# A hybrid RWKV-7 / differential-attention layer: norm weights spread by TensorE, norms and the last store in halves, scores and half a block moved in the hand-written order

## What is computed

```python
h = rmsnorm(x) * norm_mix_pre            # (544, 1024)
c = h @ w_in                             # RWKV-7 columns | q k v | two gates
A  = rwkv7(c_a)                          # token shift, decay, per-chunk matrix state
Bd = diff_attn(q, k, v)                  # 4 heads, two softmaxes per head, causal in chunks of 64
mix = sigmoid(g_a) * (A @ w_out_a) + sigmoid(g_b) * (Bd @ w_out_b)
x = x + rmsnorm(mix @ w_o) * norm_mix_post
u_g, u_v = split((rmsnorm(x) * norm_ffn_pre) @ w_ffn_in)
x = x + rmsnorm((silu(u_g) * u_v) @ w_ffn_out) * norm_ffn_post
```

## Time and profile before

| | |
|---|---|
| runs, median of three | 1002.26 us |
| profiled execution, its own time | 1004.91 us |
| its span, first to last instruction | 1003.1 us |
| mean granted TensorE clock | 0.996 |
| PE busy | 959.4 us (96%) |
| POOL busy | 549.9 us (55%) |
| DVE busy | 450.6 us (45%) |
| ACT busy | 290.3 us (29%) |
| dense matmuls in the chain that ended last | 71% of the span |

### The profile page before, as it was taken

How to read it: one execution, slowest core, us unless ns; L and a number is a source line. 1 busy time by engine, 2 the same in 40 slices (tenths; PEclk the granted TensorE clock), 3 DMA queues, 4 the chain that set the end, 5 groups by cost and what they waited for, 6 DMA issues and landing times.

```text
span 1003.1 us, 23249 instructions
## 1 busy us (share of the span) xinstructions
PE 959.4 (96%) x9424; PEld 910.9 (91%) x9424; DVE 450.6 (45%) x870; ACT 290.3 (29%) x828; POOL 549.9 (55%) x595
## 2 busy tenths in 40 slices
PE   5999999999999899889999989999999999999996
PEld 4999899988878787778899989999999999999996
DVE  5456688467744445455466653333333333100003
ACT  5225265245564233432313541111111111111101
POOL 6667899634354243243469325555555555656671
PEclk9999999999999999999999999999999999999998
DMA  8333322332223111150046322223322223223232
GB/s 252 93 86 84 85 63 72 114 109 76 78 67 93 39 47 35 55 208 28 28 122 217 94 64 63 84 85 91 95 84 84 84 85 96 81 80 95 80 95 90
DMA packets 138306, 89.76 MB, mean 89 GB/s; under 512 B 5514, under 2 KB 130160, under 8 KB 138224
## 3 DMA queue, kind: packets, MB, share of 16 engines
q1 hardware_dynamic: 129604, 73.17, 25.7%
q10 hardware_dynamic: 8620, 15.42, 4.3%
HBM read 79.39 MB, written 9.19 MB: 88 GB/s over the span
## 4 chain that ended last, share of the span: by engine, by line
PE 86%; DVE 6%; ACT 4%; POOL 2%; issue 2%; DMA 1%; ACTq 0%; DVEq 0%; SPq 0%; POOLq 0%
PE dense L1069 71%; PE side L1149 3%; PE side L1192 1%; PE side L1218 1%; POOL w_lo L770 1%; PE side L1270 1%; PE side L977 1%; PE side L910 1%; DMA xs<-in_x_prompt 1%; PE side L896 1%; POOL w_hi L765 1%; PE side L951 1%; DVE gain L1731 1%; DVE h_lo L1724 0%; PE side L1242 0%
## 5 line engine op out<-in xcount | busy, mean ns | idle before, releaser
L765 POOL TENSOR_SCALAR w_hi<-w_raw 128x256 fp32r<-128x256 f32 (+1 forms) x255 | 155.6, 629 | 348.7 <-PE dense L1069 331.1
L770 POOL TENSOR_TENSOR w_lo<-w_raw,w_hi 128x256 fp32r<-128x256 f32 (+1 forms) x255 | 323.0, 1288 | 9.8
L1069 PE MATMUL dense<-h_hi,w_hi 128*128 128x272 f32 (+2 forms) x1376 | 297.8, 295 | 2.9 <-DVE h_lo L1724 1.5
L1069 PE MATMUL dense<-h_hi,w_lo 128*128 128x272 f32 (+2 forms) x1376 | 289.3, 289 | 0.0
L1069 PE MATMUL dense<-h_lo,w_hi 128*128 128x272 f32 (+2 forms) x1376 | 288.4, 288 | 0.0
L1069 PEld LDWEIGHTS dense<-h_hi,w_hi 128*128 128x128 f32 x1376 | 217.8, 189 | 12.4 <-issue 6.9
L1069 PEld LDWEIGHTS dense<-h_lo,w_hi 128*128 128x128 f32 x1376 | 218.4, 189 | 0.0
L1069 PEld LDWEIGHTS dense<-h_hi,w_lo 128*128 128x128 f32 x1376 | 217.4, 189 | 0.0
L1069 PE MATMUL dense<-S,w_hi 128*128 128x272 f32 (+2 forms) x648 | 109.3, 289 | 0.0
L1069 PEld LDWEIGHTS dense<-S,w_hi 128*128 128x128 f32 x648 | 92.1, 188 | 0.3 <-issue 0.2
L1069 PE MATMUL dense<-S,w_lo 128*128 128x272 f32 (+2 forms) x324 | 68.2, 288 | 0.0
(11 more groups left out here) (286 smaller groups left out, 1345.4 us busy)
## 6 DMA issues: line engine op xcount, KB each, us to landing
w_raw<-in_w_ffn_in SPq DMA_DIRECT2D x44, 512.0 KB, 3.8
w_raw<-in_w_in SPq DMA_DIRECT2D x43, 512.0 KB, 3.9
w_raw<-in_w_ffn_out SPq DMA_DIRECT2D x16, 448.0 KB, 3.7
gates<-gst ACTq DMA_DIRECT2D x16, 272.0 KB, 2.1
w_raw<-in_w_ffn_out SPq DMA_DIRECT2D x8, 512.0 KB, 3.8
w_raw<-in_w_out_a SPq DMA_DIRECT2D x5, 512.0 KB, 3.5
w_raw<-in_w_o SPq DMA_DIRECT2D x5, 512.0 KB, 4.5
mb<-gates ACTq DMA_DIRECT2D x1, 2176.0 KB, 9.2
```

The source lines that it names most:

```text
L765: ins = nc.gpsimd.tensor_scalar(hi[:, q], raw[:, q], 1.0, 0.0, ALU.mult, ALU.add)
L770: ins = nc.gpsimd.tensor_tensor(lo[:, q], raw[:, q], hi[:, q].bitcast(F32), ALU.subtract)
L1069: ins = pe.matmul(acc[:, bk, 0:tn], w, r[:, t0:t0 + tn], start=first and n == 0, stop=final and n == 2)
```

## The change

Five edits.

1. `gain` is no longer loaded on all partitions. ACT's queue loads the one row of 4 KB, now ahead of `ident`. DVE sets 128 ones; PE multiplies them with the row (a contraction over one partition, 512 columns, twice), which gives the row on all partitions in two PSUM banks; DVE copies these to `gain` (two copies of 128x512). SP's queue has one 512 KB load less.
2. Both norms are multiplied in halves of 512 columns (L1761, L2064), each with a signal of its own; PE's transposes of a half wait for that half.
3. The last tile's residual and its store are made in halves.
4. In the attention the second piece of an odd head stands ahead of the scores instead of behind them.
5. In the recurrence tile the piece of dense work stands between `wu` and `e` instead of behind `e`.

```diff
@@ schedule()
-    s = [("normA", 0), ("normA", 1), ("normB", 0), ("normB", 1)] + [("normA", t) for t in range(2, NT)] + first_pair[:1]
+    s = [("gain",), ("normA", 0), ("normA", 1), ("normB", 0), ("normB", 1)] + [("normA", t) for t in range(2, NT)] + first_pair[:1]
...
         rows = [piece() + [("attP", *th)], piece()]
+        third = piece()
         if i + 1 < len(heads):
             rows[-1] += [("attC", *heads[i + 1])]
         if i + 2 < len(heads):
-            rows[-1] += [("attS", *heads[i + 2])]
-        rows += [piece() + [("attO", *th)] + ...]
+            rows[-1] += third + [("attS", *heads[i + 2])]
+            third = []
+        rows += [third + [("attO", *th)] + ...]
...
-        s += both("wu", t) + both("e", t) + filler(1) + yfin
+        s += both("wu", t) + filler(1) + both("e", t) + yfin
@@ sync
         x_load(0)
-        sp.dma_start(gain[:, :], i_["norm_mix_pre"][0].partition_broadcast(P)).then_inc(s_["gain_loaded"], 16)
...
-        for t in LATE + EARLY:
+        for t in LATE + EARLY[:-1]:
             sp.wait_ge(s_["zres"], NT + RANK[t] + 1)
             sp.dma_start(y_rows(t), z[0:TILES[t][1], t, :]).then_inc(s_["y_stored"], 16)
-        sp.wait_ge(s_["y_stored"], 16 * NT)
+        t = EARLY[-1]
+        for i, a in enumerate((0, D // 2)):
+            sp.wait_ge(s_["zres"], NT + RANK[t] + i + 1)
+            sp.dma_start(y_rows(t)[:, a:a + D // 2], z[0:TILES[t][1], t, a:a + D // 2]).then_inc(s_["y_stored"], 16)
+        sp.wait_ge(s_["y_stored"], 16 * (NT + 1))
@@ tensor
+            elif k == "gain":
+                pe.wait_ge(s_["ones_set"], 1)
+                pe.wait_ge(s_["gain_loaded"], 16)
+                for i in range(2):
+                    b = open_bank(pe, step, f"g{i}")
+                    close(pe.matmul(b[:, 0:512], xn[0:1, 2, 0:P], gain[0:1, 512 * i:512 * i + 512], start=True, stop=True),
+                          step, f"g{i}")
...
-                pe.wait_ge(s_["x_normed"], t + 1)
                 for i in range(2):
+                    pe.wait_ge(s_["x_normed"], 2 * t + i + 1)
...
-                pe.wait_ge(s_["xnorm"], RANK[t] + 1)
                 for i in range(2):
+                    pe.wait_ge(s_["xnorm"], 2 * RANK[t] + i + 1)
@@ scalar
+        act.dma_start(gain[0:1, :], i_["norm_mix_pre"][0:1, :]).then_inc(s_["gain_loaded"], 16)
         act.dma_start(ident[:, :], i_["cst"][:, K_ID:K_ID + P]).then_inc(s_["ident_loaded"], 16)
@@ vector
+        vec.memset(xn[0:1, 2, 0:P], 1.0).then_inc(s_["ones_set"], 1)
...
+            elif k == "gain":
+                for i in range(2):
+                    b = full_bank(dve, step, f"g{i}")
+                    drain(vec.tensor_copy(gain[:, 512 * i:512 * i + 512], b[:, 0:512]), step, f"g{i}")
...
                 if t == 0:
-                    dve.wait_ge(s_["gain_loaded"], 16)
+                    landed(dve, ("gain",), "g0")
+                    landed(dve, ("gain",), "g1")
...
-                V.mark(vec.scalar_tensor_tensor(out=xn[0:n, XN[t], :], in0=xs[0:n, t, :], scalar=rstd[0:n, t:t + 1],
-                                                in1=gain[0:n, :], op0=ALU.mult, op1=ALU.mult), s_["x_normed"], "x_normed")
+                for a in (0, D // 2):
+                    V.mark(vec.scalar_tensor_tensor(out=xn[0:n, XN[t], a:a + D // 2], in0=xs[0:n, t, a:a + D // 2],
+                                                    scalar=rstd[0:n, t:t + 1], in1=gain[0:n, a:a + D // 2], op0=ALU.mult,
+                                                    op1=ALU.mult), s_["x_normed"], "x_normed")
...
-                vec.scalar_tensor_tensor(out=dst[0:n, t, :], in0=z[0:n, t, :], scalar=rstd[0:n, t:t + 1],
-                                         in1=x1[0:n, t, :], op0=ALU.mult, op1=ALU.add).then_inc(s_["zres"], 1)
+                for a, m in ((0, D),) if (r, t) != (1, EARLY[-1]) else ((0, D // 2), (D // 2, D // 2)):
+                    vec.scalar_tensor_tensor(out=dst[0:n, t, a:a + m], in0=z[0:n, t, a:a + m], scalar=rstd[0:n, t:t + 1],
+                                             in1=x1[0:n, t, a:a + m], op0=ALU.mult, op1=ALU.add).then_inc(s_["zres"], 1)
```

More of the change, by code:

```diff
@@ L272, in schedule @@
         if i + 2 < len(heads):
-            rows[-1] += [("attS", *heads[i + 2])]
-        rows += [piece() + [("attO", *th)] + ([("vtok", th[0] + 1)] if th[0] < SAMPLE and th[1] == 1 else [])]
+            rows[-1] += third + [("attS", *heads[i + 2])]
+            third = []
+        rows += [third + [("attO", *th)] + ([("vtok", th[0] + 1)] if th[0] < SAMPLE and th[1] == 1 else [])]
         if th[0] < SAMPLE:
@@ L338, in fills @@
         return ["pv"]
+    if k == "gain":
+        return ["g0", "g1"]
     if k in ("normB", "zC"):
@@ L571, in encoder_kernel @@
     gate_stored = [sem(f"gate_stored{i}") for i in range(2)]
-    names = """rms_set ident_loaded x_sq x_normed x_hi cst_loaded small_loaded att_loaded gain_loaded lam_prod lam_exp
+    names = """rms_set ident_loaded x_sq x_normed ones_set x_hi cst_loaded small_loaded att_loaded gain_loaded lam_prod lam_exp
         smax sattn o_rms o_rst o_scaled o_hi_done shifted lora_a kinv shift_set rw_w rw_kk ksq ksqrt lora_g mb_loaded ga_loaded
@@ L2063, in _ @@
                 V(vec.reciprocal(rstd[0:n, t:t + 1], rms[0:n, t:t + 1]))
-                V.mark(vec.scalar_tensor_tensor(out=z[0:n, t, :], in0=x1[0:n, t, :], scalar=rstd[0:n, t:t + 1],
-                                                in1=gain2[0:n, :], op0=ALU.mult, op1=ALU.mult), s_["xnorm"], "xnorm")
+                for a in (0, D // 2):
+                    V.mark(vec.scalar_tensor_tensor(out=z[0:n, t, a:a + D // 2], in0=x1[0:n, t, a:a + D // 2],
+                                                    scalar=rstd[0:n, t:t + 1], in1=gain2[0:n, a:a + D // 2], op0=ALU.mult,
+                                                    op1=ALU.mult), s_["xnorm"], "xnorm")
             elif k == "zC":
```

## The result

The changed kernel takes 1009.99 us (median of nine runs, 1009.49 to 1011.8), the kernel before, with more runs beside it, 1003.28 (1001.57 to 1007.13). The ratio is 1.0064 with a 95% interval of 1.0052 to 1.0077: 6.4 us slower (5.2 to 7.7). Forecast were 1000.7 us and a range of 998.0 to 1003.4. The profiled execution of after took 1011.8 us with a span of 1008.8, so 3.0 us lie outside its span; before it was 1.8.

What follows compares the result with a forecast made beforehand. Time in which PE stands still or runs slow outside the full feed-forward loop was taken as the bound; -0.1 + 0.9 + 0 + 0 - 2.4 = -1.6 us took the median 1002.26 to 1000.7, range 998.0 to 1003.4.

Steps and rivals of the forecast that it cites:

- The start: Kernel start: the removed gain load is paid back to the spreading; gain 0.1 us, bounds gain 1.2 and loss 1.0.
- the rival of a late start: Start: `ident` lands behind the first weights (8.2), dense piece 2.6 us later, 1003.3 us; decides from 7.2 on; chance 0.12.
- `ident` landing past 6: Start: listed sign that the forecast is wrong; the forecast had `ident` landing at 5.6 us.
- now falls on tile 0, once as before: Start: DVE's product loses 0.85 us beside POOL's `w_hi` split, once, on tile 0's product.
- The rival that the pace rises earlier: Start: added matmuls and unbroken transposes raise PE's pace before the first dense piece; 2.5 us less, 998.2; chance 0.11.
- The second norm: Second norm: each split adds 0.24 us on DVE, lengthening PE's waits; cost 0.9 us, bounds 0.3 and 1.1.
- The last store: Kernel end: the half store only queues behind tile 0's data; nothing, bounds 0.3 gain and 0.2 loss.
- The scores: Attention: bank waits go, but the DVE and ACT softmax chain sets PE's time; 0, bounds 0.7 gain and 0.4 loss.
- scores go through: Attention: PE, not the softmax chain, sets the pace, so all 2.5 us come out; 998.2 us; chance 0.12.
- The recurrence: Recurrence: waits for ACT's copy of `wu` give 1.6 us, tile 2's later waits 0.85; gain 2.4, bounds 1.5 and 2.9.
- The slack of 0.5: Recurrence: DVE's copies of `e` end 0.5 us before the state product that reads them, so no new wait.
- covers nothing: Recurrence: the next wait replaces the removed one, so the moved half block gives 0; 1003.0 us; chance 0.08.

Runs made afterwards that it cites:

- experiment 12: Kernel before plus the gain row spread by PE, whole-row norms, PE waiting for `ident` behind the two spreading matmuls: 1001.66 us, ratio 0.9982.
- experiment 13: The whole changed kernel with PE's wait for `ident` moved behind the two spreading matmuls: 1008.56 us, ratio 1.0046 against the kernel before.
- experiment 2: Kernel before with only the first norm in halves, gain still loaded by DMA: ratio 0.9998, -0.2 us.
- experiment 10: Kernel before plus the gain row spread by PE and the first norm in halves, nothing else: 1008.44 us, ratio 1.0042.
- experiment 11: Kernel before plus the gain row spread with one matmul feeding both copies, whole-row norms, half its norm weights wrong: 1006.89 us, ratio 1.0022.
- experiment 15: Kernel before plus gain row spread ahead of the `ident` wait, half block between `wu` and `e`, third dense piece behind attention's output matmuls: 1000.26 us, ratio 0.9972.
- experiment 1: Kernel before plus only the gain row spread by PE, norms in whole rows: 1007.15 us, ratio 1.0024.
- the padded one: Kernel before with 24 already met waits added behind the last work of PE and 24 behind that of DVE: ratio 0.9992.

## Why the prediction was wrong

**1. The start (-0.1 forecast; +2.4 for the row alone, +4.2 with the halves).** Two terms failed. A spreading matmul was priced at 0.88 us and takes 1.70. The error is in how was read: a record of 0.39 us was taken for a full fp32 matmul of 272 columns with two passes, and a record is half of one. The Trainium skill (FP8 and Floating Point Precision, section TensorE Precision Notes) gives true fp32 four passes through the array; at 1.2 GHz that makes an estimate of 4 x 512 / 1200 = 1.71 us, and the trace agrees with 1.70 between the copies. Here the step that failed is the price of a term, not the order of events. The other term is `ident`: it landed at 6.2, not 5.6. That left DVE free 2.3 us late. From there the working held: 7.0 us were forecast from DVE's release to the first dense matmul, 17.30 - 10.6 = 6.7 were measured.

Behind both lies something that the prediction stated and didn't question. It wrote that PE waits for `ident` before anything else, and made its landing the rival of a late start. The wait wasn't needed there; experiment 12 prices it at 4.2 us at the first dense matmul. The rival named the right place, but its condition (a landing from 7.2 on) never came; the sign "`ident` landing past 6" did.

The size of the halves was right where POOL is idle (0.24 us a split). Beside POOL it was not: "now falls on tile 0, once as before" took the 0.85 us of the earlier trace rows as a fixed cost of one collision. It is the rest of POOL's instruction, so it depends on who begins first. In before the product began at 9.82, the split at 9.84, and the product lost 0.85; in the trace with the halved store the split lost 1.08 instead:

```profile
9.84 1.29 DVE L1765 SCALAR_TENSOR_TENSOR xn<-xs,rstd,gain 128x1024 f32<-128x1024 f32 x1
...
9.90 2.13 POOL L769 TENSOR_SCALAR w_hi<-w_raw 128x1024 fp32r<-128x1024 f32 x1 [9.46 <-DMA w_raw<-in_w_in]
```

With a lead of 0.01 or 0.02 us by its record the product lost (experiment 13, before), with one of 0.05 or more it won (the seven untouched starts). A few hundredths of a microsecond decide about 1 us of the start, and the trace of before, from which the forecast was worked out, is the one untouched start where it was lost. By the Trainium skill (SBUF — State Buffer, section Terms) DVE and GpSimd arbitrate for one pair of ports with a lock that is held for the full instruction, and the loser fully blocks. The traces agree: 0.53, 0.55 and 1.09 us of product behind the end of the split, for half and whole rows. From such a lock it follows that an instruction of DVE that is cut in two gives POOL a second chance to begin first; the prediction didn't weigh that. Where DVE has slack it costs nothing: in experiment 2 the halves met the splits too, and the time stayed.

**The rival that the pace rises earlier.** In experiments 10, 11 and 12 it did: the first dense matmul runs at the fast pace (0.39 us instead of 0.58), and the piece takes 3.0 us instead of 4.3 to 5.3. In experiment 12 the rise can be seen in the row of sixteen transposes itself (ns min/median/max, first and last start): they take 417 ns, and the last, at 11.7, takes 273.

```profile
L1150 PE MATMUL side<-ident,xn x16: 273/417/472, 8.3 to 11.7; 128*128 128x128 f32 x16
```

PE had done nothing but transposes since 8.3, and nothing at all from 6.0 to 8.3. So the prediction's argument that transposes do not raise the pace, for which it took the pace of before as a sign, doesn't hold in this trace. The other traces with the spreading have the same sixteen transposes, and in five of the eight the piece begins slowly; what decides is open. The 2.5 us that the rival put on it are not there. PE then stands longer for DVE's low parts, and tile 4's transposes start at 25.20 in experiment 10 against 25.13 in after; from the first dense matmul to them it is 6.5 us in experiment 12, with the fast piece, and 6.6 in experiment 15, with the slow one.

**2. The second norm (+0.9 forecast).** Right. 1.57 and 1.86 us of waiting were measured for 1.4 and 1.9, +0.8 and about +0.2 by stages.

**3. The last store (0 forecast).** Right: -0.1.

**4. The scores (0 forecast, bounds -0.7 and +0.4; +2.5 measured in the stage).** The removed waits did go (1.13 us for 512 columns in the odd groups). The step that failed is "that start depends on DVE, not on when the scores were ready". It was true of the old order, where DVE waited for scores twice. It was read as a law instead of as a slack, and the earlier trace rows held the slack: the scores of 262.45 end at 263.58 and DVE begins with them at 263.81, 0.2 us later; those of 266.53 end 1.0 us before 269.01. Put behind another piece they come 0.2 to 0.9 us too late, eight times, and as the prediction itself says, the softmax chain sets PE's pace. Its own argument with the condition turned round gives the loss. The rival "scores go through" had the wrong sign.

**5. The recurrence (-2.4 forecast, bounds -1.5 and -2.9).** The mechanism was right, the size too large. The direct waits and the 0.66 of tile 2 are gone. The slack of 0.5 was counted for the state product; the late reader is nearer, PE's transposes behind `e`, which wait 0.26, 0.19, 0.19 and 0.19 us for DVE's copies. In the profiled execution the four tiles give 0.0, -0.4, -1.0 and -0.3 (the issue gap of before left out), so -1.7; a new issue gap of 0.62 at 360.95 takes part of it back. The term that was mis-sized is the direct wait: 0.39 a tile was taken as gained, and 0.19 to 0.26 came back as a wait for DVE's copies. In four other traces with the edit the stage from 325 to 445 is 0.5 to 0.9 shorter, and the run alone gave -1.1. The rival "covers nothing" is what happened in tile 0.

**What no term held.** 0.8 us on average lie outside the span. And dips of the granted clock: near 27 us in the profiled execution, worth 1.5 us. Between 22 and 31 us they were seen in three of the eight traces with the spreading and in none of the others, which is too few to call the change their cause. The cause of the dips stays open, as does what remains of the +2.0 us by which the pair of experiment 10 exceeds its parts: the collision of halves and splits accounts for 0.7 to 0.9 (PE's tile 4 transposes at 25.2 instead of 24.5), the time outside for 0.3.

Nor did any term hold the 0.7 to 0.8 us that are lost near 240 us with the spreading (experiment 1): the prediction looked at the attention for edit 4 alone.

The sum with the measured sizes: 4.2 (start, both edits, with the 0.7 near 240) + 2.5 (scores) + 1.0 (second norm) - 1.1 (half block) + 0 (store) + 0.5 (more outside the span than the pair has) = 7.1, against 6.4 (5.2 to 7.7). In the attention the parts don't quite add up: from 205 to 325 us the spreading gives +0.7 and the scores +2.5, the three traces with both +2.6. The sum also rests on medians that leave 1.5 us of uncertainty, so it is partly luck that it comes out so near.

## What to carry to other kernels

That an engine doesn't wait at a step says how early its input is only after one has looked at how long the input had been ready: before a producer is moved back, read that slack for every consumer, and for the chain that sets the pace first of all. New work at the start of an in-order engine belongs ahead of the waits that it doesn't need. And an instruction of DVE that others wait for should not be cut in two while POOL has long instructions of its own, even if the cut costs only 0.24 us by itself.

## What the runs showed of the hardware

- DVE's product of two SBUF operands and POOL's splits exclude each other for a whole instruction: 0.75 us of work took 2.52, 1.28 took 2.71, and POOL's 1.04 took 2.13 when DVE had begun first. DVE's copies from PSUM took 0.69 beside a split (8.27 and 9.97 in after), as without one.
- The pace of PE rose within an unbroken row of transposes in one trace (417 ns, the last 273) and not in others with the same row.
- A full fp32 matmul of one row by 512 columns took 1.70 us at the start and leaves two records of 1.06 us each (1.22 for the first of all).
- Gaps with the releaser "issue" on PE come and go between kernels whose work at that place is the same: 1.41 us at 451.19 in before and at 449.13 with the half block alone, 1.81 in the second trace of after at the same matmul, none there in the first.
- Two programs that are longer than before, the whole change and the padded one, fetched instructions behind the end of the span, with up to 1.6 us more outside it (1.8 before, 3.4 at most).
- The kernel before ranged over 1000.5 to 1009.3 us on one chip, with the mean granted clock at 0.999 to 0.993; in these 35 runs 0.001 of granted clock goes with 0.77 us. So medians of twelve runs still leave 1.5 us of uncertainty, and the stages of a trace tell more than its time.
